# First norm of a two-block network: products with diagonals instead of scaled rows and transposes

## The reference, cut to what matters

```python
def rmsnorm(x, g):
    y = x * lax.rsqrt(jnp.mean(x * x, axis=-1, keepdims=True) + EPS)
    return y * g

def first_block(x, meta_tokens, g_pre_mix, w_in, ...):
    h = jnp.concatenate([meta, x], axis=1)          # 16 + 256 = 272 tokens
    u = rmsnorm(h, g_pre_mix)                       # the part that is changed
    z = u @ w_in
    q, k, v, xr, yr = jnp.split(z, split_at, axis=-1)
    ...                                             # window attention, LRU, output product, FFN
```

## Time and profile before

| | |
|---|---|
| median of 3 runs | 925.2 us |
| the profiled execution's own time | 924.04 us |
| its span on the core | 922.3 us |
| TensorE matmul busy | 98% of the span |
| VectorE, ScalarE, GpSimd busy | 65%, 56%, 3% |
| mean granted TensorE clock | 0.998 of full speed |

### The profile page before, as it was taken

How to read it: one execution, slowest core, us unless ns; L and a number is a source line. 1 busy time by engine, 2 the same in 40 slices (tenths; PEclk the granted TensorE clock), 3 DMA queues, 4 the chain that set the end, 5 groups by cost and what they waited for, 6 DMA issues and landing times.

```text
span 922.3 us, 16849 instructions
## 1 busy us (share of the span) xinstructions
PE 906.7 (98%) x6554; PEld 840.8 (91%) x6554; DVE 604.0 (65%) x955; ACT 518.3 (56%) x903; POOL 23.9 (3%) x36
## 2 busy tenths in 40 slices
PE   9999999999999999999999999999999999999997
PEld 7978799999997999999999999999987999999986
DVE  5688755555557566678677777765658455554576
ACT  6568654444446655657556474745549444444463
POOL 4000300000000000000000000000000000000000
PEclk9999999999999999999999999999999999999999
DMA  9823686666554454544223140515555655556541
GB/s 290 290 93 93 183 194 188 190 195 193 186 182 138 130 181 147 182 145 130 92 77 107 47 136 14 170 40 189 182 195 162 204 183 182 181 187 198 179 165 47
DMA packets 107871, 144.47 MB, mean 157 GB/s; under 512 B 2984, under 2 KB 95400, under 8 KB 107824
## 3 DMA queue, kind: packets, MB, share of 16 engines
q1 hardware_dynamic: 105648, 137.60, 46.6%
q0 software_dynamic: 1968, 6.02, 2.7%
q10 hardware_dynamic: 208, 0.20, 0.1%
HBM read 142.76 MB, written 1.05 MB: 156 GB/s over the span
## 4 chain that ended last, share of the span: by engine, by line
PE 82%; DVE 9%; ACT 5%; issue 2%; DMA 1%; POOL 0%; DVEq 0%; ACTq 0%; SPq 0%
PE ps L1685 15%; PE ps L1687 15%; PE ps L1686 15%; PE ps L1691 8%; PE ps L1693 8%; PE ps L1692 8%; PE ps L2065 2%; PE ps L2052 2%; PE ps L2069 2%; DVE R L1425 2%; DVE wl L1141 1%; ACT wh L620 1%; DVE R L1177 1%; DVE R L1192 1%; PE ps L1857 1%
## 5 line engine op out<-in xcount | busy, mean ns | idle before, releaser
L1141 DVE TENSOR_TENSOR wl<-w_raw,wh 128x1024 fp32r<-128x1024 f32 x251 | 305.2, 1224 | 218.1 <-ACT wh L620 217.3
L1685 PE MATMUL ps<-xTh,wh 128*128 128x256 f32 (+1 forms) x1160 | 334.5, 288 | 3.5 <-DVE xTl L1167 3.5
L1687 PE MATMUL ps<-xTh,wl 128*128 128x256 f32 (+1 forms) x1160 | 326.2, 281 | 0.0
L1686 PE MATMUL ps<-xTl,wh 128*128 128x256 f32 (+1 forms) x1160 | 326.1, 281 | 0.0
L620 ACT ACTIVATE wh<-w_raw 128x1024 fp32r<-128x1024 f32 x251 | 263.0, 1052 | 81.0 <-PE ps L1693 59.8
L1685 PEld LDWEIGHTS ps<-xTh,wh 128*128 128x128 f32 x1160 | 219.1, 189 | 7.5 <-issue 3.1
L1686 PEld LDWEIGHTS ps<-xTl,wh 128*128 128x128 f32 x1160 | 218.5, 188 | 1.9 <-issue 1.0
L1687 PEld LDWEIGHTS ps<-xTh,wl 128*128 128x128 f32 x1160 | 219.2, 189 | 0.0
L1691 PE MATMUL ps<-wh,y 128*128 128x512 f32 x224 | 87.9, 392 | 0.0
L1693 PE MATMUL ps<-wh,y 128*128 128x512 f32 x224 | 87.6, 391 | 0.0
L1692 PE MATMUL ps<-wl,y 128*128 128x512 f32 x224 | 87.1, 389 | 0.0
(11 more groups left out here) (360 smaller groups left out, 1335.5 us busy)
## 6 DMA issues: line engine op xcount, KB each, us to landing
w_raw<-in_w_in_dram SPq DMA_DIRECT2D x42, 1024.0 KB, 5.2
w_raw<-in_w_ff_dram SPq DMA_DIRECT2D x32, 1024.0 KB, 5.6
w_raw<-in_w_ffn_gate_dram SPq DMA_DIRECT2D x11, 1024.0 KB, 5.3
w_raw<-in_w_ffn_up_dram SPq DMA_DIRECT2D x11, 1024.0 KB, 5.4
w_raw<-in_w_ffn_down_dram SPq DMA_DIRECT2D x11, 1024.0 KB, 5.0
w_raw<-in_w_out_dram SPq DMA_DIRECT2D x8, 1024.0 KB, 5.0
w_raw<-in_w_proj_a_dram SPq DMA_DIRECT2D x4, 1024.0 KB, 5.1
w_raw<-in_w_proj_b_dram SPq DMA_DIRECT2D x4, 1024.0 KB, 5.2
```

The costliest lines, as they stand in the source:

```text
L1141: TT(low_part, raw_unit(SLOT[p], j, layout), high_part.bitcast(F32), ALU.subtract).then_inc(w_lo, 1)
L1685: mm(out, wh_, xh, start=first, stop=False)
L1686: mm(out, wh_, xl, start=False, stop=False)
L1687: return mm(out, wl_, xh, start=False, stop=last)
```

## The change

- The gain is loaded as 8 rows of 128 (row k is channels 128k to 128k+127), after the meta rows; one transpose turns it into 128 partitions by 8 columns in PSUM, and VectorE copies it to `first_gcol`. The gain of channel slice k is then one value on each partition.
- VectorE makes three diagonal matrices, identity times 1/rms, for the two tiles of x and the 16 meta rows (`first_diag`, `meta_diag`).
- A product of x (as stationary matrix) with the diagonal gives x transposed and scaled at once. Slice n goes into a bank of its own, 16 columns of meta and 256 of x, in plain float32. Eight slices take the banks in `FIRST_BANKS`; the eighth reuses bank 0 after unit 0's first step.
- The split pieces are then one per slice, 128x272, with the gain as per-partition scale: ScalarE `xTh = ps * gain`, VectorE `xTl = ps * gain - xTh`. TensorE takes a step of unit 0 as soon as its piece is there.
- VectorE squares and sums the meta rows; GpSimd keeps only its memsets and DMAs. The products of zeros ahead of the norm become one run of 22; before there were 19, in four runs.

```diff
@@ -215,6 +215,7 @@
         ps = ctx.enter_context(nc.psum_tensor("ps", [P, 8, 512], F32))
         acc, fm, ma, mb = ps[:, 0:4, :], ps[:, 4:6, :], ps[:, 6, :], ps[:, 7, :]
         high = ps[:, 4:8, :]
+        FIRST_BANKS = (0, 1, 2, 3, 5, 6, 7, 0)
 
 
         w_raw = sb("w_raw", [P, RING, 2048])
@@ -232,9 +233,10 @@
         cst = sb("cst", [P, C_END])
         ones = sb("ones", [P, P])
         zero_r = sb("zero_r", [P, P])
-        eps = sb("eps", [P, 1])
         st = sb("st", [P, 32])
+        eps = st[:, 31:32]
         nst = sb("nst", [P, 16])
+        first_gcol = sb("first_gcol", [P, KC])
 
         R = sb("R", [P, REGION])
 
@@ -252,6 +254,8 @@
 
         c1 = [0]
         u = carve(c1, NT, D)
+        first_diag = u[:, 0, 512:512 + NT * P].rearrange("p (t n) -> p t n", t=NT)
+        meta_diag = u[0:META, 1, 512:512 + META]
         meta = carve(c1, D)
         xr_pad = carve(c1, LT, T1 + 3)
         xc = carve(c1, LT, T1)
@@ -546,11 +550,6 @@
             pool.memset(xr_pad[:, :, 0:3], 0.0).then_inc(filled, 1)
             pool.memset(wa_bd[:, :, :], 0.0).then_inc(filled, 1)
             pool.memset(wx_bd[:, :, :], 0.0).then_inc(filled, 1)
-            pool.wait_ge(meta_loaded, 16)
-            pool.wait_ge(gain_first, 16)
-            pool.tensor_tensor(meta_g, meta[0:META, :], gain[0:META, 0, :], ALU.mult).then_inc(meta_steps, 1)
-            pool.wait_ge(meta_steps, 2)
-            pool.tensor_scalar(meta[0:META, :], meta_g, st[0:META, 6:7], None, ALU.mult).then_inc(meta_steps, 1)
             pool.wait_ge(filled, 6)
             pool.wait_ge(w_loaded[SLOT[P_Q + 1]], LOADS[P_Q + 1])
             for dst, name in ((wa_bd, "w_a"), (wx_bd, "w_x")):
@@ -667,24 +666,22 @@
                                ACT.Copy).then_inc(ut_hi, 1)
 
 
-            act.dma_start(gain[0:META, 0, :], A["g_pre_mix"][0].partition_broadcast(META)).then_inc(gain_first, 16)
             act.dma_start(meta[0:META, :], A["meta_tokens"]).then_inc(meta_loaded, 16)
+            act.dma_start(gain[0:KC, 0, 0:P], A["g_pre_mix"][0].rearrange("(k p) -> k p", p=P)).then_inc(gain_first, 16)
             act.dma_start(ident, A["cst"][:, C_IDENT:C_TRI]).then_inc(ident_loaded, 16)
             act.preload_act_table(ACT.Sqrt)
             act.wait_ge(filled, 4)
             for t in range(NT):
                 act.wait_ge(x_loaded[t], 16)
                 root(h[:, t, :], t)
-            act.wait_ge(meta_loaded, 16)
-            root(meta[0:META, :], 2)
-            for n in range(2):
-                piece_hi(n, META)
+            act.wait_ge(meta_steps, 1)
+            act.activation(st[0:META, 6:7], st[0:META, 2:3], ACT.Sqrt, bias=eps[0:META, 0:1], scale=1.0 / D).then_inc(stat, 1)
             hi(0)
-            for n in range(2, 4):
-                piece_hi(n, META)
-            pieces[0] += 1
-            act.wait_ge(ut_ps, pieces[0])
-            act.activation(xTh[:, :, 0:META], ma[:, 0:KC * META].rearrange("p (k n) -> p k n", k=KC), ACT.Copy).then_inc(ut_hi, 1)
+            act.wait_ge(u_ready, 2)
+            for n in range(KC):
+                pieces[0] += 1
+                act.wait_ge(ut_ps, pieces[0])
+                act.activation(xTh[:, n, :], ps[:, FIRST_BANKS[n], 0:T1], ACT.Copy, scale=first_gcol[:, n:n + 1]).then_inc(ut_hi, 1)
             for n in range(1, 4):
                 hi(n)
 
@@ -1193,28 +1190,27 @@
 
 
             dve.wait_ge(filled, 4)
-            for t in range(NT):
-                inverse(4 + t)
-                for half in range(2):
-                    if t == 0:
-                        dve.wait_ge(vec_ps, half + 1)
-                    cols_ = slice(half * 512, half * 512 + 512)
-                    STT(u[:, t, cols_], h[:, t, cols_], st[:, 4 + t:5 + t], fm[:, half, :], ALU.mult, ALU.mult).then_inc(u_ready, 1)
-            roots[0] += 1
-            dve.wait_ge(stat, roots[0])
-            dve.reciprocal(st[0:META, 6:7], st[0:META, 6:7]).then_inc(meta_steps, 1)
-            for n in range(2):
-                piece_lo(n, META)
+            dve.wait_ge(meta_loaded, 16)
+            link(TT(meta_g, meta[0:META, :], meta[0:META, :], ALU.mult))
+            dve.tensor_reduce(st[0:META, 2:3], meta_g, AX, ALU.add).then_inc(meta_steps, 1)
+            inverse(4)
+            dve.wait_ge(ident_loaded, 16)
+            TS(first_diag[:, 0, :], ident, st[:, 4:5], None, ALU.mult).then_inc(u_ready, 1)
+            dve.wait_ge(vec_ps, 1)
+            dve.tensor_copy(first_gcol[:, :], fm[:, 0, 0:KC]).then_inc(u_ready, 1)
+            inverse(5)
+            TS(first_diag[:, 1, :], ident, st[:, 5:6], None, ALU.mult).then_inc(u_ready, 1)
+            inverse(6, META)
+            TS(meta_diag, ident[0:META, 0:META], st[0:META, 6:7], None, ALU.mult).then_inc(u_ready, 1)
             lo(0)
-            for n in range(2, 4):
-                piece_lo(n, META)
-            pieces[0] += 1
-            dve.wait_ge(ut_hi, pieces[0])
-            TT(xTl[:, :, 0:META], ma[:, 0:KC * META].rearrange("p (k n) -> p k n", k=KC), xTh[:, :, 0:META].bitcast(F32),
-               ALU.subtract).then_inc(ut_lo, 1)
+            dve.wait_ge(u_ready, 2)
+            for n in range(KC):
+                pieces[0] += 1
+                dve.wait_ge(ut_hi, pieces[0])
+                STT(xTl[:, n, :], ps[:, FIRST_BANKS[n], 0:T1], first_gcol[:, n:n + 1], xTh[:, n, :].bitcast(F32), ALU.mult, ALU.subtract).then_inc(ut_lo, 1)
             for n in range(1, 6):
                 lo(n)
-            dve.wait_ge(vec_ps, 3)
+            dve.wait_ge(vec_ps, 2)
             dve.tensor_copy(cwb, mb[:, 0:8 * LT].rearrange("p (m n) -> p m n", m=LT)).then_inc(vec_out, 1)
             lo(6)
 
@@ -1790,23 +1786,37 @@
 
 
             pe.wait_ge(filled, 3)
-            zero_products(6)
+            zero_products(22)
             pe.wait_ge(gain_first, 16)
-            for half in range(2):
-                mm(fm[:, half, :], ones[0:1, :], gain[0:1, 0, half * 512:half * 512 + 512], start=True, stop=True).then_inc(vec_ps, 1)
-            zero_products(4)
             pe.wait_ge(ident_loaded, 16)
-            transposes(u, u_ready, 0)
-            zero_products(7)
-            pe.wait_ge(meta_steps, 3)
-            for k in range(KC):
-                last = pe.transpose(ma[:, k * META:(k + 1) * META], meta[0:META, k * P:(k + 1) * P], ident[0:META, 0:META])
-            last.then_inc(ut_ps, 1)
-            pieces[0] += 1
-            zero_products(2)
-
-            pieces_ready()
-            run(fm_steps(0, xTh, xTl, 0, T1))
+            pe.transpose(fm[:, 0, 0:KC], gain[0:KC, 0, 0:P], ident[0:KC, 0:KC]).then_inc(vec_ps, 1)
+
+            def first_products(n, t):
+
+                pe.matmul(ps[:, FIRST_BANKS[n], META + t * P:META + (t + 1) * P], h[:, t, n * P:(n + 1) * P], first_diag[:, t, :],
+                          start=True, stop=True)
+
+            def meta_products(n):
+
+                mm(ps[:, FIRST_BANKS[n], 0:META], meta[0:META, n * P:(n + 1) * P], meta_diag, start=True, stop=True).then_inc(ut_ps, 1)
+                pieces[0] += 1
+
+            pe.wait_ge(u_ready, 1)
+            for n in range(KC - 1):
+                first_products(n, 0)
+            pe.wait_ge(u_ready, 4)
+            for n in range(KC - 1):
+                first_products(n, 1)
+                meta_products(n)
+            steps = fm_steps(0, xTh, xTl, 0, T1)
+            for n in range(KC):
+                pe.wait_ge(ut_lo, n + 1)
+                next(steps)
+                if n == 0:
+                    for t in range(NT):
+                        first_products(KC - 1, t)
+                    meta_products(KC - 1)
+            run(steps)
             unit_ready(1)
             a, b = (split_view(w, 1, "cols") for w in (wh, wl))
             for t, (off, n) in enumerate(((META, P), (META + P, P), (0, META))):
```

## The result

The changed kernel takes 926.9 us in the median of 16 executions (926.14 to 929.85). The kernel before took 925.5 in 16 executions around them (923.89 to 925.79). The ratio is 1.0022 with a 95% interval from 1.0015 to 1.0029: 0.2% slower. Forecast were 923.8 us and a range of 922.2 to 925.4, so the result lies outside the range, on the side to which I had given 8%.

The account below looks back on a forecast made before the run. TensorE, busy 98% of the span, bounds the kernel, so only an earlier start of its real work pays. Unit 1 from 17.50 to 16.1 gains 1.4 us: 924.04 to 922.6, median 923.8; range 922.2 to 925.2, given as 925.4 with the result.

Parts of the forecast that it names:

- TensorE's zeros: Start of TensorE's list: 22 products of zeros from 1.18 us, six or seven slow to about 4.0, ending at 7.6.
- The pairs: Before unit 0: seven pairs, each an x tile 1 product and a 16-column meta product, 0.42 us each, 9.2 to 12.2.
- the pairs take over 0.5 each: Sign to look for in the profile: pairs over 0.5 us each would mean the 16-column product was priced wrongly.
- Step 0 and bank 7: Start of unit 0: step 0 takes 0.39 us, then bank 7's two products and a meta one 0.64, to 13.25.
- Identity and roots: Inputs to the diagonals: meta rows at 4.2 us, identity 6.1 to 7.8, x roots 8.3, meta root 8.6.
- The pieces: Splits ahead of unit 0's steps: VectorE's eight from 11.05 us at 0.42 each, ScalarE's 0.4 each; VectorE done by 14.5.
- The handover behind them: Unit 0 to unit 1: TensorE ready at 15.95 us, unit 1's own weight split letting it start at 16.1.
- an estimate from the figures of the Trainium skill: VectorE's pieces: PSUM source costs about 65 ns more, eight take 0.5 us more, unit 1 at 16.3, gain 1.2.
- The rest moves along: After unit 1's start: TensorE's own work or waits tied to it, shifting by the same amount, 1.4 us.
- My slower rival: Start: a late diagonal lets TensorE's clock fall and stay down; low until 15 us, a loss of 2.0, 927.2; chance 6%.
- The last step of the forecast: Whole kernel: the median stands 1.16 us above the profiled execution, so 922.6 becomes 923.8.
- GpSimd's 3.5 us: Chain before unit 0: the change takes GpSimd off the path, and with it the chain's last 3.5 us.

Follow-up runs that it names:

- e3: Changed kernel with each meta product replaced by one of the same 16 columns but 128 rows, meta tokens left out of the result: median 923.73 us.
- e2: Changed kernel with the seven meta products in a row ahead of x tile 1's products, instead of one behind each: median 925.17 us.
- e6: Changed kernel with the identity loaded ahead of the gain, 16 products of zeros instead of 22, and meta products in a row: median 923.69 us.
- e4: Changed kernel with 12 products of zeros instead of 22 and the identity loaded ahead of the gain: median 927.23 us.
- e7: Changed kernel with 32 products of zeros instead of 22: median 931.08 us.
- e5: Changed kernel with 12 products of zeros instead of 22 and the meta products in a row: median 925.76 us.
- e8 to e10: Changed kernel, identity ahead of gain; in order: 20 zeros, meta products in a row, 923.67 us; 16 zeros, meta rows transposed, 922.35; 20 zeros, transposed, 923.14.
- e1: Changed kernel with 12 products of zeros instead of 22: median 929.91 us.
- e11: Changed kernel with the identity loaded ahead of the gain and 20 products of zeros instead of 22, meta products still in pairs: median 925.92 us.

## Why the prediction was wrong

Step by step, for the start of unit 1, forecast at 16.1 and measured at 20.28:

- *TensorE's zeros: the first term that failed.* "Six or seven run slowly to about 4.0" was wrong: 13 did, to 6.9. Two merged records of the changed kernel tell the pace, 0.43 each (1.05 less the last one's 0.63) still at 5.6 us, and 0.23 at 7.5 us:

```profile
5.61 1.05 PE L1773 MATMUL ps<-zero_r 128*128 128x512 f32 x2
...
7.52 0.62 PE L1773 MATMUL ps<-zero_r 128*128 128x512 f32 x2
```

  0.43 us for 512 columns is 1.2 GHz. I had taken the moment of the rise from one execution. The run ended at 9.2, and the first diagonal product came at 9.36 instead of 7.7: 1.7 us of the 4.2. In the other profiles 22 zeros took 7.25 and 8.13 us.
- *The pairs: the largest term.* Seven at 0.42 were forecast (9.2 to 12.2), seven at 0.74 came; less the lead of tile 1's first product, that is 5.0 us instead of 3.0: 2.0 us. Tile 0's seven products add 0.2 (0.25 each instead of 0.22). I bounded the meta product from the record of two columns and from a product of 128 columns, both with 128 rows of weights, and so let it only be cheaper, never dearer. What was missing was not its price but the change of rows, which I had put at nothing: e3 restores the forecast pair (0.45), e2 the forecast product (0.24). I had even named "the pairs take over 0.5 each" as a sign.
- *Step 0 and bank 7:* 1.34 instead of 1.03, by the same cause, 0.3 us. The remaining seven steps took 2.75, forecast 2.7.
- *Identity and roots.* The identity landed at 7.9, 0.1 outside my bounds (6.1 to 7.8), and was hidden by the zeros. Meta rows at 3.8, the raw weights at 8.0 and the last root at 7.8 were earlier than forecast; none was on the path.
- *The pieces.* Right in price: VectorE 0.50, back to back 0.41 (eight in 3.36 us in e6). VectorE's pieces waited for TensorE all along. The handover behind them was right: I had put unit 1's split 0.15 behind TensorE, and it was 0.1, and 0.3 once the pairs were gone. By an estimate from the figures of the Trainium skill that I had weighed there (VectorE: DVE Perf Modes, the TRN2 errata) a piece would have taken 0.48; the row was right. That estimate was also carried on wrongly in the prediction: its own terms give unit 1 at 16.2 (11.05 + 8 x 0.485 + 1.23), not 16.3.
- *The rest moves along:* right, to 0.1 us, from 116 to 718 us.
- *The clock.* My slower rival had the wrong trigger. Where a profile shows the fall with pairs, it came not after a late diagonal but in the middle of the pairs, with TensorE busy 1.00 (e4, e7). In the changed kernel 4 of 16 executions have a mean clock of 0.996 or less, the worst at 929.85, but the profiled one does not (granted clock 1.00 in each us to 20), so the 4.2 us owe nothing to it. That the pairs make a fall likelier rests on the counts, 12 of 34 executions against 0 of 59; e5 shows that it comes without them too, with few zeros and a gap of 2.0 us. "Twice as long" at half the clock was too much for a pair: 1.27 us against 0.74 in e4. My reading of the Trainium skill (TensorE: Matmul & The Clock Gate, What's actually happening), that a gapless run of zeros would hold the clock up, failed here: 32 zeros did not protect the pairs behind them.

Sum: 1.7 for the zeros, 0.2 for tile 0's products, 2.0 for the pairs and 0.3 for step 0 and bank 7 make 4.2 us, which turns a forecast gain of 1.4 at unit 1 into a loss of 2.8; the profiled executions differ by 2.6, the medians by 1.4. The last step of the forecast, that the median stands 1.16 above the profiled execution, failed as well: it stands 0.3 above it in the changed kernel. That made the miss look smaller than the error of the mechanism, which is luck. GpSimd's 3.5 us did leave the path; e6 and e8 to e10 show the gain that this opens.

Open stays why the executions of the kernel before fall into two groups, 924.1 and 925.7, the quicker with the lower mean clock (0.996 to 0.998 against mostly 0.998 to 1.0); I suppose the rise comes earlier in the quick ones, but no execution of the slower group was profiled. Open is also the fall at 705 to 711 us in the profiled executions of e3 and e6 (mean clock from 700 to 710: 0.85 and 0.83), which the other profiled executions do not have; what decides it was not tried.

## What to carry to other kernels

On TensorE's path count a product at the price that it has behind its neighbour: alternating weights of few and of 128 rows cost 0.3 us a pair here, and putting the small ones in a row, or making them transposes, gives it back. Price a warm-up by its slowest execution, not by one profile, look at the spread of times and clocks before the median, and find out in a profile where in the span the clock fell: e1 made the profiled execution 1.45 us faster and the median 3 us slower. When an engine leaves the path, ask first which engine's own list is long enough to take it over.

## What the runs showed of the hardware

- Weights of 16 rows after weights of 128 rows, and the reverse, are not loaded ahead: pair 0.74 us, against 0.45 with 128 rows in both. The Trainium skill (TensorE: Matmul & The Clock Gate, The mechanism) says in one line that a weight load overlaps with products in flight only when its row group differs, and in another that one into the background weight buffer is pulled ahead too. The trace of e3 agrees with the second: its loads of the same 128 rows run ahead of their products, by up to 0.1 us. In the changed kernel loads that change from 128 to 16 rows or back don't.
- A busy share of 1.00 does not keep the clock: it fell from 2.4 to 1.2 GHz during such pairs (e4 at 12 us, e7 at 17 us). In the profiled executions of the changed kernel, e1 and e11 the same pairs ran without a fall.
- The granted clock in the windows reads 1.00 while products still run at the 1.2 GHz pace, from the start to the first rise (0.43 us for 512 columns at 5.6 us, window 5 to 6 at 1.00). The length of products tells the clock there, the column does not.
